# A top-2-of-8 expert SwiGLU in groups of 32 tokens: four column lanes for every width, 32x32 turns on VectorE, quarter-row gathers and writes, weight rows of 4 KB

## The reference, cut to what matters

```python
top_logit, top_e = lax.top_k(logits, 2)          # 384 tokens, 8 experts
gates = jax.nn.softmax(top_logit, axis=-1)
# each token's row goes to its two experts; for expert e, rows xb:
(silu(xb @ wg[e]) * (xb @ wu[e])) @ wd[e]        # wg, wu 1024x2816, wd 2816x1024
# y[token] = sum over its two experts of gate * row; x += modulation gate * y
```

## Time and profile before

| | us |
|---|---|
| median of 3 runs | 1914.96 (1911.09 to 1916.73) |
| the profiled execution's own time | 1909.48 |
| its span | 1907.7 |
| TensorE busy | 1842.8 (97%) |
| VectorE, ScalarE, GpSimd busy | 545.0, 398.3, 114.2 |
| bytes moved by DMA | 427.26 MB, 224 GB/s over the span |

### The profile page before, as it was taken

The page is one execution under the profiler, slowest core; times in us unless marked ns, Lnnn a source line. Parts: engine busy times, 40 slices in busy tenths (PEclk is TensorE's granted clock), DMA queues, the critical chain, the costliest instruction groups (busy, mean ns, idle before and its releaser), DMA issues.

```text
span 1907.7 us, 31785 instructions
## 1 busy us (share of the span) xinstructions
PE 1842.8 (97%) x13719; PEld 1290.4 (68%) x13719; DVE 545.0 (29%) x1189; ACT 398.3 (21%) x901; POOL 114.2 (6%) x112
## 2 busy tenths in 40 slices
PE   7999999999999999998989999999999999999998
PEld 4654655889999887554775454568644456879695
DVE  2640336235455102165352000201012110111033
ACT  2221227110001001353231110311113121212021
POOL 0000111000000000000001001110020101020200
PEclk9999999999999999999999999999999999999999
DMA  8722237246552334234266556998689999999991
GB/s 317 275 101 97 79 114 262 89 142 211 177 155 62 113 112 175 74 133 141 90 241 216 206 189 202 392 384 319 211 274 392 384 395 376 365 362 364 327 381 62
DMA packets 232974, 427.26 MB, mean 224 GB/s; under 512 B 16693, under 2 KB 87700, under 8 KB 232510
## 3 DMA queue, kind: packets, MB, share of 16 engines
q1 hardware_dynamic: 218496, 411.65, 60.8%
q0 software_dynamic: 10192, 11.74, 1.8%
q10 hardware_dynamic: 4142, 1.72, 0.3%
HBM read 425.77 MB, written 26.51 MB: 237 GB/s over the span
## 4 chain that ended last, share of the span: by engine, by line
PE 89%; DMA 3%; DVE 3%; issue 2%; SPq 1%; ACT 1%; ACTq 0%; POOL 0%; POOLq 0%; DVEq 0%
PE bank L1134 25%; PE bank L612 11%; PE bank L853 11%; PE bank L1301 6%; PE bank L1227 6%; PE bank L905 6%; PE bank L662 4%; PE bank L1165 2%; PE bank L727 2%; DMA ring<-in_moe_w_gate_dram 2%; PE bank L517 2%; PE bank L948 1%; SPq L2603 1%; PE bank L576 1%; PE bank L937 1%
## 5 line engine op out<-in xcount | busy, mean ns | idle before, releaser
L1134 PE MATMUL bank<-ring,HTXN 128*32 128x384 f32 (+3 forms) x3104 | 290.0, 395 | 7.7 <-issue 6.2
L1395 ACT ACTIVATE arena<-bank 128x512 f32<-128x512 f32 (+4 forms) x323 | 143.2, 505 | 579.9 <-PE bank L853 175.6
L1134 PEld LDWEIGHTS bank<-ring,HTXN 128*32 128x32 f32 (+2 forms) x3104 | 204.3, 120 | 86.7 <-issue 63.5
L1134 PE MATMUL bank<-arena,HTXN 128*32 128x384 f32 (+3 forms) x2336 | 223.8, 394 | 5.4 <-DVE HTXN L2300 3.1
L1134 PEld LDWEIGHTS bank<-arena,HTXN 128*32 128x32 f32 (+2 forms) x2336 | 156.9, 122 | 66.2 <-issue 47.0
L2363 DVE TENSOR_TENSOR arena<-arena,bank 128x512 f32<-128x512 f32 x120 | 76.8, 684 | 416.2 <-PE bank L1134 376.9
L612 PE MATMUL bank<-ring,HTXN 128*128 128x512 f32 (+4 forms) x528 | 153.0, 452 | 1.0 <-DVE HTXN L2185 1.0
L1740 ACT ACTIVATE arena<-bank 128x512 f32<-128x512 f32 x120 | 65.0, 597 | 379.2 <-PE bank L1134 317.6
L612 PEld LDWEIGHTS bank<-ring,HTXN 128*128 128x128 f32 x528 | 96.2, 190 | 57.1 <-issue 47.2
L853 PE MATMUL bank<-HTXN,arena 128*128 128x192 f32 x704 | 121.4, 326 | 0.0
L905 PE MATMUL bank<-ring,arena 128*128 128x256 f32 x528 | 114.2, 379 | 2.6 <-DVE arena L2112 2.6
(11 more groups left out here) (375 smaller groups left out, 1857.8 us busy)
## 6 DMA issues: line engine op xcount, KB each, us to landing
ring<-in_moe_w_up_dram SPq DMA_DIRECT2D x53, 1024.0 KB, 14.1
ring<-in_moe_w_gate_dram SPq DMA_DIRECT2D x49, 1024.0 KB, 9.5
ring<-in_w_mod_dram SPq DMA_DIRECT2D x24, 2048.0 KB, 9.0
ring<-in_moe_w_down_dram SPq DMA_DIRECT2D x48, 1024.0 KB, 7.8
arena<-in_moe_w_down_dram SPq DMA_DIRECT2D x40, 1024.0 KB, 12.0
arena<-in_moe_w_gate_dram SPq DMA_DIRECT2D x39, 1024.0 KB, 11.7
arena<-in_moe_w_up_dram SPq DMA_DIRECT2D x35, 1024.0 KB, 8.5
ring<-in_w_in_dram SPq DMA_DIRECT2D x10, 2048.0 KB, 10.4
```

Source lines behind the costliest of these rows:

```text
L1134: last = mm(bank[row:row + rows_, col:col + cn], xe[:, i, k, at:at + rows_], wt[:, c0:c0 + cn], start=(k == 0 and col == 0), stop=(k == KT ...
L1395: return act_fn(out, in_, ACT.Copy)
```

## The change

All widths are now counted in groups of 32 rows (2, 3, 4, 5, 6, 8 or 12), at most 4 groups to a piece. Each 128-input step of each group is four products, one in each 32-column lane; a lane takes a quarter of the columns in hand. The hidden columns go in three blocks of 1024, 1024 and 768, so a lane has 256, 256 or 192 columns. A down step is 22 times four products of 256 columns, and results lie as quarter rows: lane q holds columns 256q to 256q+255 of its 32 rows. A piece fills two PSUM banks at once.

VectorE turns the products by 32x32 blocks (`v.transpose`) from `sgm` to `act_a`, and the gathered rows from `xrow` to `xe`. TensorE's transposes of rows and products and ScalarE's copies of them are gone. The rows are gathered as quarter rows, one indirect DMA for each of 12 groups of a turn, and written by 12 more. The weights come in 35 chunks a turn: two rows of 4 KB to a partition (3 KB in the third block) for gate and up, and 8 KB in one piece for down, with the inputs dealt to partitions in another order to match. Absent pieces are filled as before. ScalarE now copies all results of a turn except the last. For the last turn the slot table is made on VectorE from six TensorE transposes, the results are multiplied by the modulation gates while they are drained, and 12 products of 32 rows by 256 columns per token tile and three groups bring them to tokens.

```diff
-WIDTHS = [64, 96, 128, 160, 192, 256, 384]
+G_OF = [2, 3, 4, 5, 6, 8, 12]
+WIDTHS = [32 * g for g in G_OF]
+NPIECE, PGROUPS = 3, 4
+NJ = [256, 256, 192]
...
+        MOE_FILLS = [(s, j, i) for j in range(3) for s in ("g", "u") for i in range(NPIECE)]
+        for n, label in enumerate(MOE_FILLS + [("y", 0), ("y", 1), ("y", 2)]):
+            b = n % 4 if n < len(MOE_FILLS) else (2, 3, 1)[n - len(MOE_FILLS)]
+        MOE_CHUNKS = ([(s, j, kp) for j in range(3) for s in ("g", "u") for kp in range(4)]
+                      + [("d", j, cp) for j in range(3) for cp in range(NJ[j] // 64)])
...
+            def hidden(e, groups, kind, j, pieces, last_use=True):
+                banks = {i: moe_fill((kind, j, i), e) for i in pieces}
+                here = [gi for gi in range(groups) if gi // PGROUPS in pieces]
+                n = NJ[j]
+                for kp in range(4):
+                    pe.wait_ge(*moe_landed((kind, j, kp), e))
+                    wt = moe_part((kind, j, kp), e, 4 * n)
+                    for k in (2 * kp, 2 * kp + 1):
+                        for gi in here:
+                            bank, full = banks[gi // PGROUPS]
+                            at = 256 * (gi % PGROUPS)
+                            for q in range(4):
+                                last = mm(bank[32 * q:32 * q + 32, at:at + n], xe[:, gi, k, :], wt[:, k % 2, q * n:(q + 1) * n],
...
+            def output(e, groups):
+                for n, (_, j, cp) in enumerate(MOE_CHUNKS[-NDN:]):
+                    if n == 2 and e < LAST:
+                        absent(e, groups, [("y", i) for i in range(NPIECE)])
+                    if n == 6 and e == LAST:
+                        late_tables(e)
...
+                                for q in range(4):
+                                    last = mm(banks[i][0][32 * q:32 * q + 32, QD * g:QD * g + QD], act_a[:, at:at + 32],
+                                              wt[:, c % 2, QD * q:QD * q + QD], start=(n == 0 and c == 0 and g % 2 == 0),
...
+                act_fn(sgm[:, i, :, 0:NJ[j]], by_group(moe_banks_of(("g", j, i)), j), ACT.Silu).then_inc(moe_drained(("g", j, i), e)[0], 1)
...
             def product(j, i, e):
...
+                v.tensor_tensor(a, a, by_group(moe_banks_of(("u", j, i)), j), ALU.mult).then_inc(moe_drained(("u", j, i), e)[0], 1)
...
+                v.transpose(act_a[:, act_at(j, i):act_at(j, i) + c * P].rearrange("p (g c t) -> p g c t", g=PGROUPS, c=c),
+                            sgm[:, i, :, 0:NJ[j]].rearrange("p g (r c) -> p g c r", c=c)).then_inc(act_ready, 1)
...
+            def turn_rows(i, e):
+                dve.wait_ge(xrow_loaded[i], 16 * PGROUPS * (e if i == 0 else e + 1))
+                v.transpose(xe[:, PGROUPS * i:PGROUPS * (i + 1), :, :],
+                            xrow[:, PGROUPS * i:PGROUPS * (i + 1), :].rearrange("p g (r c) -> p g c r", c=KT)).then_inc(xe_ready, 1)
...
             def gather_rows(e, i):
+                for g in range(PGROUPS * i, PGROUPS * (i + 1)):
+                    g_.indirect_dma_start(xrow[:, g, :], None, x_quarters, at_row(8 + NE * g + e),
...
             def write_out(e, i):
+                pool.wait_ge(*moe_drained(("y", i), e))
+                for g in range(PGROUPS):
+                    g_.indirect_dma_start(y_quarters, at_row(8 + NE * (PGROUPS * i + g) + e), yt[:, i, g, :], None,
...
+                src = src.rearrange("a (p c) n -> p (a c) n", p=P)[:, 2 * hk:2 * hk + 2, :]
+                sp.dma_start(mslot[n % MRING][:, 0:2 * width].rearrange("p (k n) -> p k n", k=2), src).then_inc(mslot_full[n % MRING], 16)
```

More of the change, by code:

```diff
@@ L1100, in turn_rows @@
-            def turn_rows(e, i, after):
-                for q in range(2):
-                    bank, full = moe_fill(("X", i, q), after)
-                    if q == 0:
-                        pe.wait_ge(xrow_loaded[i], 16 * (e if i == 0 else e + 1))
-                    for k in range(4):
-                        last = tp(bank[:, k * P:(k + 1) * P], xrow[:, i, (4 * q + k) * P:(4 * q + k + 1) * P], ident)
-                        if k == 0:
-                            settle(last)
-                    last.then_inc(full, 1)
@@ L1220, in _ @@
-            OUT_96 = ([(0, 32 * n, 0, n, 0, 512) for n in range(3)] + [(0, 96, 0, 0, 768, 256), (0, 96, 256, 1, 768, 256)]
-                      + [(1, 32 * n, 0, n, 512, 256) for n in range(3)] + [(1, 96, 0, 2, 768, 256)])
-            def output_96(bank0, bank1, a, wt, f):
-                for b, row, col, group, c0, cn in OUT_96:
-                    bank, full = (bank0, bank1)[b]
-                    last = mm(bank[row:row + 32, col:col + cn], a[:, 32 * group:32 * group + 32], wt[:, c0:c0 + cn],
-                              start=(f == 0 and col == 0), stop=(f == FT - 1 and (b == 1 or row < 96 or col > 0)))
-                    if f == 0 and (b, row) == (0, 0):
-                        settle(last)
-                    if f == FT - 1 and row == 96 and (b == 1 or col > 0):
-                        last.then_inc(full, 1)
-                return last
@@ L1235, in slot_tables @@
-            def slot_tables(e, w):
-                pe.wait_ge(slots_ready, 1)
-                for n, label in enumerate(TABLES):
-                    bank, full = moe_fill(label, e)
-                    lanes = range(4) if n == 0 else [3] if w == 96 else []
-                    if not lanes:
-                        pe.sem_inc(full, 1)
-                        continue
-                    for t in range(NT):
-                        for lane in lanes:
-                            c = 32 * n if w == 96 and lane == 3 else 32 * lane % w
-                            last = mm(bank[32 * lane:32 * lane + 32, t * P:(t + 1) * P], slots[:, t, c:c + 32], ident,
-                                      start=(t == 0), stop=(t == NT - 1))
-                    last.then_inc(full, 1)
@@ new lines, in _ @@
+                if e < LAST:
+                    for i in range(NPIECE):
+                        turn_rows(i, e + 1)
+            dve.wait_ge(y_written, 16 * NGROUP * LAST)
+            for q in range(4):
+                note(v.tensor_copy(gate_q[32 * q:32 * q + 32, :, :], GB[32 * q:32 * q + 32, :, QD * q:QD * q + QD]))
+            dve.wait_ge(*moe_filled(("y", 1), LAST))
+            tables = moe_banks_of(("y", 1))
+            then(v.tensor_copy(gate_by_token, tables[:, 512:512 + TOK]))
+            for g in range(PGROUPS):
+                last = v.scalar_tensor_tensor(slot_t[:, g, :], tables[:, 0:TOK], place_of[:, g:g + 1], gate_by_token, ALU.is_equal, ALU.mult)
@@ new lines, in _ @@
+            last.then_inc(moe_drained(("y", 1), LAST)[0], 1)
+            for t in range(NT):
+                dve.wait_ge(late_loaded[t], 16)
+                add_rows(late_y, gl_before, t)
+            dve.wait_ge(dve_step, steps[0])
+            dve.wait_ge(*moe_filled(("y", 0), LAST))
+            for s in range(2):
+                v.tensor_tensor(y_gated[s], moe_banks_of(("y", 0))[:, :].rearrange("p (g n) -> p g n", g=PGROUPS),
+                                gate_q[:, s, :].unsqueeze(1).broadcast_to([P, PGROUPS, QD]), ALU.mult).then_inc(y_gated_ready, 1)
```

611 lines of the change are left out of this document (187 added, 424 removed).

## The result

| | before | after |
|---|---|---|
| median, us | 1913.34 (4 runs, 1911.09 to 1916.73) | **2005.59** (4 runs, 1999.5 to 2009.06) |
| span of the profiled execution | 1907.7 | 2006.4 |
| experts, first to last product | 891.45 | 991.6 (1003.38 to 1994.98) |

The ratio is 1.0477, 95% interval 1.0443 to 1.0511: slower by 92 us, where 1880 was forecast. The two profiled executions differ by 98.7 us, and all of it lies in the expert part: 100.1 us more there, 1.5 us more ahead of it, and 3.0 us less in the tail (11.4 against 14.4).

A forecast was written before the change was run, and what follows sets the result against it. TensorE's own products were taken as the bound: 821.4 + 29.3 + 3 + 5 + 1.2 = 859.9 us against 891.45, with edges of -0.4 and -2.7 making -34.6. Forecast 1880 us, range 1850 to 1904 (0.8 of the cases).

The forecast's parts named there:

- GpSimd, "Cost nothing": Row gathers and writes: 24 indirect DMAs a turn, 31 us against 64 of the shortest turn, rows there in time, no cost.
- Starts of a turn: TensorE after each branch: instructions arrive late for short products; 3.9 us for seven starts, 2 for the first, 29.3 us.
- Straight code: TensorE inside the turn bodies: stalls among many short products, 3 us over all turns, ends 0 and 20.
- The products: TensorE in the expert part: full steps at 0.4425 us and short ones at 0.34, together 821.4 us, ends 793 and 833.
- VectorE: 32x32 turns priced as products (1.22 us, short 0.95); TensorE waits in the two 64-row turns, 5 us in all.
- dear turns: Rival: VectorE's 32x32 turns at twice the price, losses in short and 96-row turns, up to +19 us, 1899; chance 0.14.
- Weights: Weight DMAs in the turns: 398 GB/s with longer rows; DMA waits go, the time of a short turn stays.
- Edges: Before and after the experts: slot tables 1.2 us, routing -0.4, first strided weight loads covered, tail 11.7 us (-2.7).
- Slower: instructions: Rival: TensorE's expert code, instructions late while weights fill the queues, 0.005 us a product, 39 us, 1919; chance 0.08.

The follow-up runs named there:

- e1: The changed kernel without the 176 indirect DMAs that gather and write rows inside the turns (output not the reference's): 1867.19 us, 0.9769 of the kernel before.
- e7: e5 with no work on absent pieces in the loops of ScalarE, VectorE and the bank list: 1878.53 us, 0.9805 of the kernel before.
- e2: The changed kernel with indirect DMAs only for groups that hold rows in this routing, 49 in place of 176, same bytes: 1891.27 us, 0.9908.
- e5: The changed kernel with fixed slots for rows, moved by plain DMAs on SyncE between the weights, absent rows too: 1884.44 us, 0.9827.
- e12: e7 with each weight DMA split into two halves of its columns, rows of 2 KB (1.5) in place of 4 KB (3): 1896.08 us, 0.9882.
- e4: The kernel before the change with 84 more indirect writes, 12 a turn, into tables nobody reads: 1942.21 us, 1.0161 of the kernel before.
- e15: e5 plus 84 indirect DMAs of 32 rows each on GpSimd to scratch tables, bound 0 so nearly all rows are left out: 1962.78 us.
- e14: e5 plus 84 indirect DMAs of 128 rows each on GpSimd to scratch tables, bound 0 so nearly all rows are left out: 1934.01 us.
- e18: The kernel of e8 measured again in another session, all rows in bounds: 1942.04 us, with the kernel before at 1912.81 beside it.
- e6: The fixed slots and plain row DMAs of e5, issued by GpSimd in place of SyncE: 1878.74 us (one run).
- e8: e5 plus 84 indirect DMAs of 128 rows on GpSimd to scratch tables, all in bounds: 1886.52 us, with the kernel before at 1899.01 beside it.
- e11: e7 with rows moved by GpSimd's plain DMAs in place of SyncE's: 1876.77 us, with the kernel before at 1899.01 beside it.

## Why the prediction was wrong

Wrong in its sign: 2006 for 1880, outside 1850 to 1904. e1 separates the step that failed from those that held: without the rows' DMAs the kernel takes 1867, and its expert part 848.8 us, where the prediction had 859.9.

- **GpSimd, "Cost nothing": the step that failed.** It counted the 24 indirect DMAs a turn as GpSimd's own time and asked only whether the rows would be late. TensorE never waited for them. What they cost is TensorE's supply of instructions: 142.8 us in the expert part (991.6 - 848.8). No term of the sum had a place for one engine's instruction slowing another's.
- **Starts of a turn, 29.3: right rows, wrong cause.** The earlier trace rows was read as the branch's price. The timelines of GpSimd and TensorE in the kernel before, laid side by side only now, have five indirect DMAs from 1604.4 to 1610.6, the first and the last of them being

```profile
1604.36 0.98 POOL L2493 DMA_INDIRECT expert_out<-arena,idx  x1 [5.46 <-DMA expert_out<-arena,idx]
...
1609.55 1.01 POOL L2476 DMA_INDIRECT HTXN<-expert_rows,idx  x1 [0.30 <-issue]
```

  and the broken records of TensorE beside them:

```profile
1607.87 1.71 PE L1134 MATMUL bank<-arena,HTXN 128*32 128x384 f32 x10 [0.17 <-issue]
1610.04 0.28 PE L1134 MATMUL bank<-arena,HTXN 128*32 128x128 f32 x1 [0.45 <-issue]
```

  From 3 us after the first DMA of a burst of five to 2 us after the last, 5.2 us, TensorE ran 37, 38 and 37 records beside 96-row pieces (bursts at 1258.5, 1604.4, 1703.3; 77 to 94 in the 5 us before the first two); in a 64-row turn (1198.6) 50, where the 5 us before had 46, and in the 128-row turn (1486.2) 13 and 13. That is why only the 96-row turns seemed to start badly. What the branch itself costs is 11.9 us over seven starts (e1), not 29.3.
- **Straight code, 3: too small.** e1 has 6.9 us of "issue" inside the bodies. Indirect DMAs aren't the cause of 6.5 of them, with GpSimd idle, nor of the stall of the earlier trace rows, beside which GpSimd's timeline is empty from 1640 to 1670 us; what is stays open.
- **The products, 821.4: over by 6.** In e1 848.8 less 18.8 of issue, 13.9 of VectorE and 0.9 for the tables leaves 815. Steps of 256 columns took 0.4355 (0.4425 forecast), short ones 0.329 (384 records in 15.81 us, 0.34 forecast). At these rates it would be 806; the other 9 us lie where records come more slowly, as after the branch at 1672.84 (288 records in 17.43 us, elsewhere 15.75). The upper end of this sum was 831, not 833.
- **VectorE, 5: mis-sized.** A 32x32 turn of 1024 columns takes 2.08 us, not 1.22 (768: 1.59, not 0.95); a product 1.20, as priced. TensorE waits 13.9 us in e1, at the places named (third piece's bank in short turns, and in the down part). The rival "dear turns" was nearer to the turn's size (twice 1.22); it comes to 9 us more, not 19. Bounding the absent pieces (e7) takes these waits away.
- **Weights:** right for the bytes of the change: no wait is left in it, nor in e1 and e2, whose expert parts (848.8 and 870.7) lie about the forecast 859.9. It is a near thing: with the 17.5 MB more of e5 TensorE waits 11.5 us for weights, in e7 18.8. The rates are 416 against 383 GB/s by e7 and e12; 402 and 384 were read in the earlier trace rows. The Trainium skill ("DMA: Bandwidth & Descriptors", Where 436 GB/s comes from) puts a core's share of HBM, a stack's rate halved between two cores, at about 358; e7's stretch, with one core at work, is 58 above it.
- **Edges:** the tail is 11.4 us for 11.7, the row lanes overlap. The strided weight loads of the first gathered rows were not free: L1055 took 11.7 us for 48 records, with 336 ns for a weight load, against 5.6 us and 192 ns before; TensorE's first product came 1.5 us late, and the 3.15 us wait of the earlier trace rows is gone into it. TensorE's tail:

```profile
1996.48 2.87 PE L1167 MATMUL banks<-arena 32*128 32x256 f32 x48 [1.51 <-DVE arena L2207]
1999.59 1.58 PE L1167 MATMUL banks<-arena 32*128 32x256 f32 x24 [0.23 <-DVE X L2214]
```

- **The rival "Slower: instructions"** had the place, TensorE's dense code, but its condition was weights filling the queues. The stretch of 1016 to 1038 us has 8 GB/s. Its 39 us were a quarter of the loss. The earlier trace rows showed late instructions, and they were charged to branch and code without a run that tried either.

The change with its DMAs made plain is worth what was forecast of it: e5 to e7 at 1878 to 1884 us, 34 to 40 under the kernel beside them. In part that is luck. In e1 the starts come out 17 us under their charge and the products 6, VectorE's waits 9 and the straight code 4 over, and e5 and e7 add waits for weights that the sum put at nothing.

## What to carry to other kernels

A stall put down to "issue" has a cause that the profile doesn't name: lay the timelines of all other engines beside it, GpSimd's first, before it is booked as a price of the code. When a change multiplies one kind of instruction, double that kind in the old kernel and time it (e4's 84 writes would have shown +33 us, 30 of them in the expert part), even where its own engine has time to spare. Keep indirect DMAs out of stretches in which TensorE works on narrow products: fewer and larger ones, plain ones at fixed slots, or beside wide products.

## What the runs showed of the hardware

- Indirect DMAs of GpSimd cut TensorE's instruction supply from 18.7 records per microsecond to 2 to 11 (bursts of four and more), from about 3 us after the first to 2 us after the last, also with the DMA queues nearly empty. A write of 32 rows costs no less than one of 128 (e15, e14, out of bounds), and one of 128 rows in bounds no less than one out of bounds (e18, e14). Plain DMAs of GpSimd don't do it (e6). Products of 128 rows at 2.3 records per microsecond don't feel it (the 128-row turn: 116.81 us with and without e4's additions).
- In one session (e8 to e11) this price was absent, and the kernel before was 11 to 20 us faster too. Cause open.
- The granted clock falls to the 1.2 GHz level in such a stretch and stays there for at least 3 us after it.
- Weights in DMAs of 1 MB with rows of 4 KB (and 3) come at 416 GB/s, in DMAs of half the size with rows of 2 KB (and 1.5) at 383.
- VectorE turns 128x1024 float32 elements by 32x32 blocks in 2.08 us, 1.7 times a product of the same size that reads PSUM (1.20).
